# First head pair's queries and keys made by seven block products behind the gates, in a hybrid encoder layer

## The chip, the cores and the metric

The kernel runs on one core of a Trainium2 chip. The metric is the device time of one execution in microseconds. It is the median of three runs for the kernel before: 1119.58 us (1119.29 to 1119.91). A profile is one more execution, with its own time.

## The reference

One layer of a post-norm encoder for 1024 tokens of 1024 channels in float32. It has two sub-layers; the change touches the first, and in it the two branches below.

```python
proj = x @ w_in[l] + b_in[l]
glu_in, q, k, v, gate_logits = jnp.split(proj, splits, axis=-1)
y_conv = conv_branch(glu_in, w_dw[l], b_dw[l], ln_conv_g[l], ln_conv_b[l], w_conv_out[l])
y_attn = chunked_attention(heads(q), heads(k), heads(v), rel_bias[l]) @ w_attn_out[l]
g_conv, g_attn = jnp.split(jax.nn.sigmoid(gate_logits), N_BRANCHES, axis=-1)
mixed = (g_conv * y_conv + g_attn * y_attn) @ w_o[l] + b_o[l]
x = layer_norm(ALPHA * x + mixed, ln1_g[l], ln1_b[l])
x = layer_norm(ALPHA * x + grouped_moe(...), ln2_g[l], ln2_b[l])
```

`conv_branch` is a GLU (512 channels), a causal depthwise convolution of width 31, a LayerNorm over the channels (mean, centring, variance), a swish and a product. `chunked_attention` has 8 heads of 64 channels, a band of 640 key columns for a tile of 128 queries, and a learned bias.

## The kernel before, in words

Every large product is made in three parts, with each operand split in a high and a low half: `mm3` (lines 685 to 687) issues high by high, low by high and high by low. ScalarE makes the high half (`high`, `unit_high`), VectorE or GpSimd subtracts it to get the low half (`low`, `unit_low`, `first_low`, `v_low`, `qk_low`). The order of the work is written out by hand: each engine has its own program, and semaphores tie them.

TensorE's program, in order:

1. Blocks 0 to 7 (128 weight columns each): the GLU halves, `weights_left`. Meanwhile VectorE runs the 31 taps of the convolution, channel block by channel block (`conv_tap`, line 1245), and the last channel block's GLU product is `glu(3)` (line 1229).
2. The gates: 2048 columns as 8 pairs of column blocks. Each pair is made by 7 block products ("units") in place of 8, with sums of weight blocks and of token blocks (Strassen's scheme in Winograd's form). 56 units, `gate_product`, of 12 matmuls each. Each unit needs a weight block of 256 KB in one of 8 slots (`load_unit` on SP's queue), split by ScalarE and by GpSimd (L647). The sums of weight blocks are made by DMAs on GpSimd's queue, from DRAM to DRAM, in rounds: `sums_round(r)` waits until all of round r-1 has landed, and issues the copies (L634) and the accumulating DMAs (L632) of its stages. Rounds 0 to 4 stand before the first `unit_low`; round 5 stands behind that of unit 4, round 6 behind that of unit 9 (`LATE_ROUNDS`). VectorE adds the products up (`gate_sums`, L1289) between taps, ScalarE takes the sigmoid and SP stores the gates.
3. The convolution's mean (`conv_mean`, line 745: two products with ones), then the values of two head pairs in 8 tiles of 24 matmuls (`v_tile`), with the variance (`conv_var`, line 753) ahead of tile 5.
4. Queries and keys of the first head pair, blocks 10 and 11, by 4 `half_sum`s of 24 matmuls of 512 columns.
5. The attention in 32 slots (`scores` L779, `transpose_probs` L793, `weigh_values` L807), with the other pairs' queries and keys, the other values and the convolution's output product between. Then the output products and the mixture of experts.

In stage 3, VectorE centres (line 1367), sums the squares (1259), and makes the low halves of the values (1354). Behind the values come four reciprocals (1376), `normalise` (1349) and the low halves of the first pair (1362). GpSimd makes the low halves of blocks 8 to 11 (L603), scales and masks two bias tiles (`scale_bias`, L609 to L613), then the low halves of blocks 12 and 13. Four PSUM banks serve the value tiles: tile t waits for `v_lo` of tile t-4. Behind the values TensorE waits for the block and for the last tile's low half:

```python
for i in range(2):
    pe.wait_ge(w_lo, B_Q[0] + i + 1)
    pe.wait_ge(v_lo, TT)
```

## Time and profile before

| | |
|---|---|
| median of 3 runs | 1119.58 us (1119.29 to 1119.91) |
| the profiled execution | 1120.55 us, its span 1118.8 us |
| TensorE matmuls | 1081.1 us busy, 97% |
| VectorE, ScalarE, GpSimd | 833.2, 556.9, 365.0 us busy |
| chain that ended last | TensorE 81%, VectorE 6%, DMA 4%, ScalarE 3% |

The span leaves out 1.75 us of the profiled execution. A matmul's duration overlaps with the next one's, so the pace of a series is the distance between starts. A row's time in brackets is the idle time of the engine ahead of it, with what ended it; "issue" stands where nothing in the profile did. In a row with a count, the duration is that of the whole series.

### The profile page before, as it was taken

The page shows a single profiled execution, that of the slowest core. Times are in us where ns is not written, and L with a number is a line of the kernel's source. Part 1 is how long each engine was busy: PE and PEld are TensorE (multiplying, and loading weights), DVE is VectorE, ACT ScalarE, POOL GpSimd, SP SyncE. Part 2 cuts the span into 40 slices and gives each one's busy share as a digit, 9 for nine tenths or more (in the row PEclk, how much of TensorE's full clock was granted, in tenths as well). Part 3 has the DMA queues.
Part 4 walks back from the last instruction along what each step waited for, and adds up shares of the span by engine and source line. Part 5 has one row for each costly group of instructions (what it writes and reads, how often), then busy time and mean ns, then how long its engine had stood idle before and what let it go on. Part 6 is the DMA issues. An engine that isn't in the chain of part 4 may idle for free.

```text
span 1118.8 us, 17230 instructions
## 1 busy us (share of the span) xinstructions
PE 1081.1 (97%) x5487; PEld 897.1 (80%) x5488; DVE 833.2 (74%) x1195; ACT 556.9 (50%) x854; POOL 365.0 (33%) x317
## 2 busy tenths in 40 slices
PE   9999999999999999999999999899999999999984
PEld 7887888888788889788888888788888888888762
DVE  7899999995667766666774688888588646548766
ACT  6412343434476755645330224487487545548764
POOL 2535454444176854667000000024122121112220
PEclk9998999999999999999999999999999999999998
DMA  9898555543201100450750435898999975699966
GB/s 324 252 232 192 162 161 147 159 145 104 75 20 43 31 33 7 183 225 23 269 188 1 157 149 204 304 329 313 377 325 365 317 250 183 205 382 327 348 206 243
DMA packets 60938, 222.68 MB, mean 199 GB/s; under 512 B 9169, under 2 KB 9553, under 8 KB 56770
## 3 DMA queue, kind: packets, MB, share of 16 engines
q1 hardware_dynamic: 51602, 182.49, 44.0%
q0 software_dynamic: 9264, 39.27, 14.5%
q8 instruction: 40, 0.66, 0.2%
q14 instruction: 32, 0.26, 0.1%
HBM read 189.27 MB, written 49.30 MB: 213 GB/s over the span
## 4 chain that ended last, share of the span: by engine, by line
PE 81%; DVE 6%; DMA 4%; ACT 3%; issue 3%; POOL 2%; DVEq 1%; ACTq 0%; SPq 0%; POOLq 0%
PE ps L685 15%; PE ps L687 15%; PE ps L686 15%; PE ps L1823 8%; PE ps L1825 8%; PE ps L1824 8%; PE ps L807 2%; PE ps L793 2%; DMA dn_raw<-in_wexp 2%; DMA gu<-in_wexp 2%; PE ps L779 2%; PE ps L1904 1%; PE ps L1819 1%; POOL pr L597 1%; PE ps L1931 1%
## 5 line engine op out<-in xcount | busy, mean ns | idle before, releaser
L1722 DVE TENSOR_TENSOR gu<-gu (+1 forms) x128 | 148.5, 1219 | 34.7 <-issue 20.8
L1245 DVE SCALAR_TENSOR_TENSOR ps<-u,dw_t,ps 128x1024 f32<-128x1024 f32 x116 | 149.1, 1285 | 2.3
L1823 PE MATMUL ps<-gu,xgh 128*128 x336 | 134.0, 399 | 3.4 <-DVE xgl L2221 2.8
L1716 ACT ACTIVATE gu<-gu (+1 forms) x128 | 124.0, 1047 | 21.7 <-DMA gu<-in_wexp 13.6
L1825 PE MATMUL ps<-gu,xgl 128*128 x336 | 131.7, 392 | 0.0
L1824 PE MATMUL ps<-gu,xgh 128*128 x336 | 131.4, 391 | 0.0
L597 POOL TENSOR_SCALAR pr<-pr,rinv 128x640 f32<-128x640 f32 (+4 forms) x64 | 95.4, 1503 | 77.3 <-DVE rinv L1407 77.1
L685 PE MATMUL ps<-xh,wh 128*128 128x512 f32 x256 | 102.9, 402 | 1.7 <-DVE vhl L1354 1.0
L686 PE MATMUL ps<-xl,wh 128*128 128x512 f32 x256 | 100.0, 390 | 0.0
L687 PE MATMUL ps<-xh,wl 128*128 128x512 f32 x256 | 99.8, 390 | 0.0
L647 POOL TENSOR_TENSOR ul<-uraw,uh 128x512 fp32r<-128x512 f32 x52 | 68.6, 1436 | 71.4 <-ACT uh L1030 71.4
L2316 DVE TENSOR_TENSOR dn_l<-dn_raw,dn_h 128x1024 fp32r<-128x1024 f32 x60 | 69.5, 1219 | 10.9 <-ACT dn_h L2064 10.8
L1823 PEld LDWEIGHTS ps<-gu,xgh 128*128 128x128 f32 x336 | 63.4, 189 | 17.4 <-issue 4.8
L1825 PEld LDWEIGHTS ps<-gu,xgl 128*128 128x128 f32 x336 | 63.4, 189 | 13.5
L1824 PEld LDWEIGHTS ps<-gu,xgh 128*128 128x128 f32 x336 | 63.6, 189 | 12.7
L1823 PE MATMUL ps<-dn_h,hbh 128*128 128x512 f32 x168 | 68.3, 407 | 2.4 <-DVE hbl L2320 2.4
L1760 POOL DMA_INDIRECT acc_rows<-ys,to_now x20 | 37.6, 1880 | 94.0 <-ACT ys L2089 77.6
L1825 PE MATMUL ps<-dn_h,hbl 128*128 128x512 f32 x168 | 66.6, 397 | 0.0
L1824 PE MATMUL ps<-dn_l,hbh 128*128 128x512 f32 x168 | 66.5, 396 | 0.0
L1120 ACT ACTIVATE pr<-pr,nmx 128x640 f32<-128x640 f32 (+4 forms) x64 | 44.1, 690 | 43.8 <-DVE nmx L1398 43.8
L1747 POOL COPY id_now<-ids_i 128x1 int32 (+1 forms) x19 | 11.3, 594 | 164.9 <-PE ps L1904 164.9
L2064 ACT ACTIVATE dn_h<-dn_raw 128x1024 fp32r<-128x1024 f32 x60 | 58.7, 1048 | 8.9 <-DMA dn_raw<-in_wexp 5.2
(308 smaller groups left out, 2662.3 us busy)
## 6 DMA issues: line engine op xcount, KB each, us to landing
gu<-in_wexp SPq DMA_DIRECT2D x64, 1024.0 KB, 8.8
dn_raw<-in_wexp SPq DMA_DIRECT2D x16, 2048.0 KB
raw<-in_wblk SPq DMA_DIRECT2D x36, 512.0 KB, 4.3
gate_weight_sums<-in_wblk POOLq DMA_DIRECT2D x48, 256.0 KB, 6.2
uraw<-gate_weight_sums SPq DMA_DIRECT2D x32, 256.0 KB, 2.9
gate_cols<-gst SPq DMA_DIRECT2D x32, 256.0 KB, 3.3
uraw<-in_wblk SPq DMA_DIRECT2D x24, 256.0 KB, 2.9
xf<-acc_rows SPq DMA_DIRECT2D x8, 512.5 KB, 8.3
```

Source lines behind the costliest of these rows:

```text
L597: pool.tensor_scalar(pr[n % 3][:, h, 0:nt * P], pr[n % 3][:, h, 0:nt * P], rinv[:, n % 3, h:h + 1], None, ALU.mult).then_inc(p_ready, 1)
L647: pool.tensor_tensor(ul[:, s], uraw[:, s], uh[:, s], ALU.subtract).then_inc(u_lo, 1)
L685: pe.matmul(o, a_h, b_h, start=first, stop=False)
L686: pe.matmul(o, a_h, b_l, start=False, stop=False)
L687: return pe.matmul(o, a_l, b_h, start=False, stop=last)
L1245: dve.scalar_tensor_tensor(out=so_far if k < CW - 1 else cv[:, j, :], in0=tap, scalar=w, in1=so_far, op0=ALU.mult, op1=ALU.add).then_inc(c ...
L1716: eng.activation(gu[:, par, k, 0, :], gu[:, par, k, 1, :].bitcast(F32), ACT.Copy).then_inc(gu_hi, 1)
L1722: eng.tensor_tensor(gu[:, par, k, 1, :], gu[:, par, k, 1, :].bitcast(F32), gu[:, par, k, 0, :], ALU.subtract).then_inc(gu_lo, 1)
L1823: pe.matmul(o, a_h, b_h, start=first, stop=False)
L1824: pe.matmul(o, a_h, b_l, start=False, stop=False)
L1825: return pe.matmul(o, a_l, b_h, start=False, stop=last)
L2316: dve.tensor_tensor(dn_l[:, k, :], dn_raw[:, k, :], dn_h[:, k, :], ALU.subtract).then_inc(dn_lo, 1)
```

## The change

The first pair's queries and keys become a ninth pair behind the eight of the gates, so that there are 63 units. Their weight sums are a fifth group of the rounds: round 4 has 4 copies more, round 5 two accumulating DMAs more, round 6 one, and a round 7 with one stands behind unit 14. Their results stand in SBUF (`gst`), not in PSUM; `qk_high` and `qk_low` of the first pair read them there, between the value tiles. The 4 half sums and their two waits go. `conv_mean` stands ahead of unit 59, and `centre`, `square` and `square_sum` between the last units. `conv_var` stands ahead of value tile 2. On VectorE the reciprocals stand behind value tiles 2 and 3, and a `normalise` behind each of tiles 4 to 7. TensorE waits for `v_lo` of all 8 tiles and for the root of the variance ahead of the first scores. `glu(3)` stands ahead of the low halves of units 2 and 3 instead of behind three taps. The slots of the units are turned by one, so that units 1, 3 and 5 wait for one block more. GpSimd splits blocks 8 to 11 and scales both bias tiles; the splits of the second pair's blocks are now those of 10 and 11. The blocks are renumbered, since two are gone.

```diff
-VAR_TILE = 5
+VAR_TILE = 2
 CCE_ROW = 2048
 FIRST_UNITS = 4
-LATE_ROUNDS = {4: 5, 9: 6}
+LATE_ROUNDS = {4: 5, 9: 6, 14: 7}
...
-B_V = (8, 16)
-B_Q = (10, 12, 14, 18)
-B_OC, B_OA, B_WO = 20, 24, 28
-N_BLOCKS = 36
+B_V = (8, 14)
+B_Q = (None, 10, 12, 16)
+B_OC, B_OA, B_WO = 18, 22, 26
+N_BLOCKS = 34
 W_GATE = N_BLOCKS
+GATE_PAIRS = KC
+Q0K0 = KC
+N_PAIRS = KC + 1
...
-UNITS = [(x, q) for q in range(KC) for x in ORDER]
+UNITS = [(x, q) for q in range(N_PAIRS) for x in ORDER]
 N_UNITS = len(UNITS)
+FIRST_SLOT = -N_UNITS % UNIT_SLOTS
...
-    cols += [v, v + 1, q, k, q + 1, k + 1, q + 2, k + 2, v + 2, v + 3, q + 3, k + 3]
-    return cols, [gate + j for j in range(N_GATE)]
+    cols += [v, v + 1, q + 1, k + 1, q + 2, k + 2, v + 2, v + 3, q + 3, k + 3]
+    return cols, [gate + j for j in range(N_GATE)] + [q, k]
...
+        def unit_slot(m):
+
+            return (m + FIRST_SLOT) % UNIT_SLOTS
+
         def sum_round(x, q):
 
             return q // 2 + {5: 1, 7: 1, 6: 2, 3: 3}[x]
 
         def sums_issued(r):
 
-            return sum(2 * many for g in range(KC // 2) for stage, many in enumerate((4, 2, 1, 1)) if g + stage <= r)
+            return sum(pairs_of(g) * many for g in range(SUM_GROUPS) for stage, many in enumerate((4, 2, 1, 1)) if g + stage <= r)
...
-        V_BANKS = (0, 1, 2, 3)
+        FROM_SLOT = (0, 2, 1, 3)
+        V_BANKS = (1, 2, 3, 4)
...
-                        sp.wait_ge(blk_used, B_V[0] - RING + m // 2 + 1)
+                        sp.wait_ge(blk_used, B_V[0] - RING + unit_slot(m) // 2 + 1)
...
-                for n in range(B_V[0], B_Q[0] + 2):
+                for n in range(B_V[0], B_Q[1] + 2):
                     low(n)
                 scale_bias(0)
                 scale_bias(1)
-                for n in range(B_Q[1], B_Q[1] + 2):
-                    low(n)
...
-                    bank_read(N_UNITS - 2)
-                    bank_read(N_UNITS - 1)
                     pe.wait_ge(sum_ok, 2 * (CB - 1))
                     for h in range(2):
-                        last = pe.matmul(ps[:, 4 + h, :], ones[:], sqr[:, 0, HALF * h:HALF * h + HALF], start=True, stop=True)
+                        last = pe.matmul(ps[:, 6 + h, :], ones[:], sqr[:, 0, HALF * h:HALF * h + HALF], start=True, stop=True)
...
+                    if m == N_UNITS - 4:
+                        conv_mean()
                     gate_product(m)
 
-                conv_mean()
...
-                for i in range(2):
-                    pe.wait_ge(w_lo, B_Q[0] + i + 1)
-                    pe.wait_ge(v_lo, TT)
-                    for h in range(2):
-                        half_sum(B_Q[0] + i, h, ps[:, 2 * i + h, :], 0, KC).then_inc(qk_done, 1)
+                pe.wait_ge(v_lo, TT)
+                pe.wait_ge(sq_done, CB + 1)
...
+                def square(j):
+                    act.wait_ge(cent, j + 1)
+                    act.activation(sqr[:, j, :], cv[:, j, :], ACT.Square).then_inc(sq_done, 1)
...
+                    if N_UNITS - 2 <= m < N_UNITS:
+                        square(2 * (m - N_UNITS + 2))
+                        square(2 * (m - N_UNITS + 2) + 1)
...
-                    act.wait_ge(qk_done, i + 1)
-                    act.activation(dst[:, HALF * h:HALF * h + HALF], o, ACT.Identity,
-                                   bias=b_in_t[:, col:col + 1]).then_inc(qk_hi, 1)
-
-                for j in range(CB):
-                    act.wait_ge(cent, j + 1)
-                    act.activation(sqr[:, j, :], cv[:, j, :], ACT.Square).then_inc(sq_done, 1)
+                    if i < 4:
+                        act.wait_ge(blk_used, B_V[0] + N_UNITS)
+                        act.wait_ge(c_sum, sum_no((C11, C12, C21, C22)[i], Q0K0))
+                    else:
+                        act.wait_ge(qk_done, i - 3)
+                    if i in (2, 3):
+                        act.activation(o, o, ACT.Identity, scale=-1.0, bias=b_in_t[:, col:col + 1]).then_inc(sig_ready, 1)
+                        act.wait_ge(sig_ready, CB + len(SIGMOIDS) + i - 1)
+                        act.activation(dst[:, HALF * h:HALF * h + HALF], o, ACT.Copy).then_inc(qk_hi, 1)
+                    else:
+                        act.activation(dst[:, HALF * h:HALF * h + HALF], o, ACT.Identity,
+                                       bias=b_in_t[:, col:col + 1]).then_inc(qk_hi, 1)
+
                 for t in range(TT):
                     v_high(0, t, ps[:, V_BANKS[t % 4], 0:2 * P])
-                    if t == 1:
-                        high(B_Q[0])
+                    if t < 4:
+                        qk_high(t, gst[:, 0, FROM_SLOT[t], :])
                     if t == 3:
-                        high(B_Q[0] + 1)
+                        high(B_Q[1])
+                    if t == 5:
+                        high(B_Q[1] + 1)
                     if t == VAR_TILE:
                         act.wait_ge(stat_done, 2)
-                        act.activation(std[:], psf[:, 4 * HALF:6 * HALF], ACT.Sqrt, scale=1.0 / DC, bias=eps[:]).then_inc(sq_done, 1)
-                high(B_Q[1])
-                high(B_Q[1] + 1)
+                        act.activation(std[:], psf[:, 6 * HALF:8 * HALF], ACT.Sqrt, scale=1.0 / DC, bias=eps[:]).then_inc(sq_done, 1)
                 for j in range(CB):
                     act.wait_ge(nrm, j + 5)
                     act.activation(cv[:, j, :], cv[:, j, :], ACT.Silu, scale=cpar[:, 1, j:j + 1],
                                    bias=cpar[:, 2, j:j + 1]).then_inc(silu_done, 1)
-                for i in range(4):
-                    qk_high(i, ps[:, i, :])
...
+                def centre(j):
+                    dve.wait_ge(stat_done, 1)
+                    dve.scalar_tensor_tensor(out=cv[:, j, :], in0=psf[:, 6 * HALF:8 * HALF], scalar=-1.0 / DC, in1=cv[:, j, :],
+                                             op0=ALU.mult, op1=ALU.add).then_inc(cent, 1)
...
+                    if n == B_V[0] - 1:
+                        glu(CB - 1)
...
-                glu(CB - 1)
                 for m in range(N_UNITS):
                     gate_sums(m)
                     some_taps(1 + (m % 2 or m < 12))
-                assert taps == CB * CW
+                    if N_UNITS - 4 <= m < N_UNITS - 2:
+                        assert taps == CB * CW
+                        centre(2 * (m - N_UNITS + 4))
+                        centre(2 * (m - N_UNITS + 4) + 1)
+                    if m == N_UNITS - 2:
+                        square_sum(1)
+                square_sum(2)
+                square_sum(3)
...
+                    if i in (2, 3):
+                        dve.tensor_tensor(lo[b % 2][:, c], o, hi[b % 2][:, c], ALU.subtract).then_inc(qk_lo, 1)
+                    else:
+                        dve.scalar_tensor_tensor(out=lo[b % 2][:, c], in0=o, scalar=b_in_t[:, col:col + 1],
+                                                 in1=hi[b % 2][:, c], op0=ALU.add, op1=ALU.subtract).then_inc(qk_lo, 1)
+
                 for t in range(TT):
-                    if 1 <= t <= 3:
-                        square_sum(t)
                     v_low(0, t, ps[:, V_BANKS[t % 4], 0:2 * P])
-                dve.wait_ge(sq_done, CB + 1)
-                for i in range(4):
-                    c = slice(2 * P * i, 2 * P * i + 2 * P)
-                    dve.reciprocal(rstdc[:, c], std[:, c]).then_inc(nrm, 1)
-                for j in range(CB):
-                    normalise(j)
-                for i in range(4):
-                    qk_low(i, ps[:, i, :])
+                    if t < 4:
+                        qk_low(t, gst[:, 0, FROM_SLOT[t], :])
+                    if t in (2, 3):
+                        dve.wait_ge(sq_done, CB + 1)
+                        for i in (2 * t - 4, 2 * t - 3):
+                            c = slice(2 * P * i, 2 * P * i + 2 * P)
+                            dve.reciprocal(rstdc[:, c], std[:, c]).then_inc(nrm, 1)
+                    if 4 <= t:
+                        normalise(t - 4)
...
+    def in_ring(i):
+        return i if i < 4 else 4 + (B_WO + i) % RING
```

VectorE's program from the last units' products (L1289, after L1310) to the first scores (ISA). Before:

```order
L1253 TENSOR_TENSOR csum<-csum,cv 128x1024
L1289 TENSOR_TENSOR gst<-ps,gst 128x512
L1367 SCALAR_TENSOR_TENSOR cv<-ps,cv 128x1024 x4
...
L1259 TENSOR_TENSOR sqr<-sqr 128x1024
L1354 TENSOR_TENSOR vhl<-ps,vhl 128x2x128 x5
L1376 RECIPROCAL rstdc<-std 128x256 x4
L1349 TENSOR_TENSOR cv<-cv,rstdc 128x1024 x4
L1362 SCALAR_TENSOR_TENSOR ql_77<-ps,b_in_t,qh_75 128x512 x2
L1362 SCALAR_TENSOR_TENSOR kl_81<-ps,b_in_t,kh_79 128x512 x2
L1398 ISA pr_86,nmx<-ps,bias_84 128x128
```

After the change, from value tile 2 on:

```order
L1388 TENSOR_TENSOR vhl<-ps,vhl 128x2x128
L1397 TENSOR_TENSOR kl_81<-gst,kh_79 128x512
L1410 RECIPROCAL rstdc<-std 128x256 x2
L1388 TENSOR_TENSOR vhl<-ps,vhl 128x2x128
L1397 TENSOR_TENSOR kl_81<-gst,kh_79 128x512
L1410 RECIPROCAL rstdc<-std 128x256 x2
L1388 TENSOR_TENSOR vhl<-ps,vhl 128x2x128
L1383 TENSOR_TENSOR cv<-cv,rstdc 128x1024
...
L1383 TENSOR_TENSOR cv<-cv,rstdc 128x1024
L1388 TENSOR_TENSOR vhl<-ps,vhl 128x2x128
L1383 TENSOR_TENSOR cv<-cv,rstdc 128x1024
L1430 ISA pr_86,nmx<-ps,bias_84 128x128
```

Where the 8 value tiles' subtractions stood ahead of the reciprocals and of `normalise`, four reciprocals and three `normalise` (L1383) now stand ahead of the last of them.

GpSimd's program from the first low half of a unit (L664) to the first probabilities (L614), after the change:

```order
L664 TENSOR_TENSOR ul<-uraw,uh 128x512
L649 DMA gate_weight_sums<-in_wblk 32x2048 x2
L649 DMA gate_weight_sums<-gate_weight_sums 32x2048 x4
L664 TENSOR_TENSOR ul<-uraw,uh 128x512 x5
L649 DMA gate_weight_sums<-gate_weight_sums 32x2048 x3
...
L620 TENSOR_TENSOR wl<-raw,wh 128x1024 x4
L626 TENSOR_SCALAR bias_84<-bias_84 128x1280
...
L626 TENSOR_SCALAR bias_85<-bias_85 128x1280
...
L614 TENSOR_SCALAR pr_86<-pr_86,rinv 128x128 x2
```

Between the low halves of units 4 and 5 there were four DMAs, and are now six. The two block splits that stood behind the bias tiles are now the last two of the four ahead of them.

## Rows read from the trace of the kernel before

**Rows 1.** The page: the chain that ended last, shares of the span by engine.

```profile
PE 81%; DVE 6%; DMA 4%; ACT 3%; issue 3%; POOL 2%; DVEq 1%; ACTq 0%; SPq 0%; POOLq 0%
```

**Rows 2.** Timeline of PE: from unit 53 to the first value tile.

```profile
245.42 0.39 PE L685 MATMUL ps<-xh,uh 128*128 128x512 f32 x1
...
253.35 0.39 PE L687 MATMUL ps<-xraw_r,ul 128*128 128x512 f32 x1
254.93 1.96 PE L745 MATMUL ps<-csum,ones 128*128 128x512 f32 x4 [1.18 <-DVE csum L1253]
256.32 0.69 PE L685 MATMUL ps<-wh,xh 128*128 128x256 f32 x1
256.84 0.28 PE L686 MATMUL ps<-wl,xh 128*128 128x256 f32 x1
```

**Rows 3.** Timeline of PE: first half sum of the first pair, and first scores.

```profile
282.64 0.47 PE L685 MATMUL ps<-xh,wh 128*128 128x512 f32 x1 [1.03 <-DVE vhl L1354]
...
304.58 0.33 PE L779 MATMUL ps<-kh,qh 64*128 64x128 f32 x2
```

**Rows 4.** Timeline of PE, then stretches of 5 us with the granted clock (PEclk), at units 1 and 2.

```profile
103.68 0.77 PE L685 MATMUL ps<-t_h,uh 128*128 128x512 f32 x1 [2.70 <-issue]
...
100.00:105.00 5.00, 2.30 (x8) 1.65 (x7) 4.93 (x5) 0.88 (x2) 1.62 (x3) 0.80 0.97 283
105.00:110.00 5.00, 5.00 (x13) 3.89 (x13) 4.96 (x6) 1.51 (x3) 5.00 (x7) 0.52 0.88 143
```

**Rows 5.** Timeline of DVE at the same place.

```profile
97.26 1.28 DVE L1263 TENSOR_TENSOR ul<-uraw,uh 128x512 fp32r<-128x512 f32 x2
...
102.30 1.28 DVE L1229 SCALAR_TENSOR_TENSOR u<-ps,b_in_t,sig 128x1024 f32<-128x1024 f32 x1
```

**Rows 6.** Timeline of POOL: rounds 3 to 5 of the weight sums.

```profile
66.44 3.92 POOL L634 DMA_DIRECT2D gate_weight_sums<-in_wblk  x8 [10.45 <-DMA gate_weight_sums<-gate_weight_sums]
...
89.34 3.16 POOL L632 DMA_DIRECT2D gate_weight_sums<-in_wblk  x4 [12.57 <-DMA gate_weight_sums<-gate_weight_sums]
...
99.57 1.29 POOL L647 TENSOR_TENSOR ul<-uraw,uh 128x512 fp32r<-128x512 f32 x1 [3.89 <-ACT uh L1030]
104.24 3.21 POOL L632 DMA_DIRECT2D gate_weight_sums<-gate_weight_sums  x4 [3.38 <-DMA gate_weight_sums<-gate_weight_sums]
106.33 3.67 POOL L647 TENSOR_TENSOR ul<-uraw,uh 128x512 fp32r<-128x512 f32 x2
```

**Rows 7.** Timeline of ACT in the value tiles: one tile, the root, a block's high half.

```profile
268.43 0.39 ACT L1084 ACTIVATE vhl<-ps 128x256 fp32r<-128x256 f32 x1 [2.50 <-PE ps L687]
...
276.30 1.28 ACT L1106 ACT_TABLE_LOAD   x1
277.59 1.11 ACT L1106 ACTIVATE std<-ps,eps 128x1024 f32<-128x1024 f32 x1
...
286.62 1.06 ACT L1020 ACTIVATE wh<-raw 128x1024 fp32r<-128x1024 f32 x1 [0.20 <-DMA raw<-in_wblk]
```

**Rows 8.** Timeline of DVE, reciprocals and `normalise`; then the latter's own durations (min/median/max).

```profile
282.41 6.58 DVE L1376 RECIPROCAL rstdc<-std 128x256 f32<-128x256 f32 x4
289.02 6.80 DVE L1349 TENSOR_TENSOR cv<-cv,rstdc 128x1024 f32<-128x1024 f32 x4
...
L1349 DVE TENSOR_TENSOR cv<-cv,rstdc x4: 1210/1211/3398, 289.0 to 294.6; 128x1024 f32<-128x1024 f32 x4
```

**Rows 9.** Timeline of POOL: a bias tile and two block splits.

```profile
272.31 3.47 POOL L609 TENSOR_SCALAR bias<-bias 128x1280 f32<-128x1280 f32 x1
...
286.57 4.76 POOL L603 TENSOR_TENSOR wl<-raw,wh 128x1024 fp32r<-128x1024 f32 x2 [6.17 <-ACT wh L1020]
```

**Rows 10.** DVE and POOL at a late split, and POOL's pair of the same size earlier.

```profile
460.67 2.67 DVE L1215 TENSOR_TENSOR wl<-raw,wh 128x1024 fp32r<-128x1024 f32 x1
...
462.24 2.80 POOL L597 TENSOR_SCALAR pr<-pr,rinv 128x256 f32<-128x256 f32 x2
...
310.09 1.83 POOL L597 TENSOR_SCALAR pr<-pr,rinv 128x256 f32<-128x256 f32 x2 [0.27 <-DVE rinv L1407]
```

More of the change, by code:

```diff
@@ L312, in wait_used @@
             elif n < B_OC:
-                b, i = [(b, n - B_Q[b]) for b in range(PAIRS) if 0 <= n - B_Q[b] < 2][0]
-                eng.wait_ge(qk_done, 1 + max(p for p in range(4 * PAIRS) if qk_of(p)[:2] == (b, i)))
+                b, i = [(b, n - B_Q[b]) for b in range(1, PAIRS) if 0 <= n - B_Q[b] < 2][0]
+                eng.wait_ge(qk_done, -3 + max(p for p in range(4 * PAIRS) if qk_of(p)[:2] == (b, i)))
             elif n < B_OA:
@@ L331, in gate_weights, with pairs_of @@
             return whole[P * DC * k:P * DC * k + P * DC]
+        SUM_GROUPS = (N_PAIRS + 1) // 2
+        def pairs_of(g):
+            return min(2, N_PAIRS - 2 * g)
+        def unit_slot(m):
+            return (m + FIRST_SLOT) % UNIT_SLOTS
         def sum_round(x, q):
@@ L359, in sigmoids_at @@
             x, q = UNITS[m - 2]
+            if q == Q0K0:
+                return []
             return [(q, slot) for after, slot in ((7, 3), (2, 0), (3, 2), (4, 1)) if after == x]
@@ L421, in oc_pieces @@
             return of
-        SPLITS = {1: (14,), 2: (15,), 5: (16,), 9: (17,), 13: (18,), 17: (19,), 25: (20,), 27: (21,), 29: (22,), 30: (23,),
-                  31: (24,), 32: (25,), 33: (26,)}
+        SPLITS = {1: (12,), 2: (13,), 5: (14,), 9: (15,), 13: (16,), 17: (17,), 25: (18,), 27: (19,), 29: (20,), 30: (21,),
+                  31: (22,), 32: (23,), 33: (24,)}
         UO_SLOTS = {23: (0,), 24: (1, 2), 25: (3,)}
@@ L543, in _ @@
                     if n == B_OA - 2:
-                        sp.wait_ge(qk_done, 4 * PAIRS)
+                        sp.wait_ge(qk_done, 4 * (PAIRS - 1))
                         sp.wait_ge(v_done, 2 * TT)
@@ L621, in weight_sums @@
                 def weight_sums(g, stage):
-                    if not 0 <= g < KC // 2:
+                    if not 0 <= g < SUM_GROUPS:
                         return
-                    for q in (2 * g, 2 * g + 1):
+                    for q in range(2 * g, 2 * g + pairs_of(g)):
                         s1, s2, s3, s4 = (wsum_dram[i, q] for i in range(4))
@@ L643, in unit_low @@
                 def unit_low(m):
-                    s = m % UNIT_SLOTS
+                    s = unit_slot(m)
                     pool.wait_ge(u_hi, m + 1)
@@ L720, in gate_product @@
                     x, q = UNITS[m]
-                    s, bank = m % UNIT_SLOTS, unit_bank(m)
+                    s, bank = unit_slot(m), unit_bank(m)
                     pe.wait_ge(u_lo, m + 1)
@@ L898, in qk_sum @@
                         pe.wait_ge(w_lo, B_Q[b] + i + 1)
-                        if p == 5:
-                            pe.wait_ge(cent, CB)
-                        elif p not in (4, 15):
+                        if p not in (4, 5, 15):
                             pe.wait_ge(qk_lo, p)
@@ L1261, in first_low @@
                 def first_low(m):
+                    s = unit_slot(m)
                     dve.wait_ge(u_hi, m + 1)
-                    dve.tensor_tensor(ul[:, m], uraw[:, m], uh[:, m], ALU.subtract).then_inc(u_lo, 1)
+                    dve.tensor_tensor(ul[:, s], uraw[:, s], uh[:, s], ALU.subtract).then_inc(u_lo, 1)
                 def input_sums():
@@ L1361, in qk_low @@
                     dve.wait_ge(qk_hi, i + 1)
-                    dve.scalar_tensor_tensor(out=lo[b % 2][:, c], in0=o, scalar=b_in_t[:, col:col + 1],
-                                             in1=hi[b % 2][:, c], op0=ALU.add, op1=ALU.subtract).then_inc(qk_lo, 1)
-                dve.wait_ge(stat_done, 1)
-                for j in range(CB):
-                    dve.scalar_tensor_tensor(out=cv[:, j, :], in0=psf[:, 6 * HALF:8 * HALF], scalar=-1.0 / DC, in1=cv[:, j, :],
-                                             op0=ALU.mult, op1=ALU.add).then_inc(cent, 1)
+                    if i in (2, 3):
[3 more added lines that the diff above has]
+                                                 in1=hi[b % 2][:, c], op0=ALU.add, op1=ALU.subtract).then_inc(qk_lo, 1)
                 for t in range(TT):
-                    if 1 <= t <= 3:
-                        square_sum(t)
                     v_low(0, t, ps[:, V_BANKS[t % 4], 0:2 * P])
-                dve.wait_ge(sq_done, CB + 1)
-                for i in range(4):
-                    c = slice(2 * P * i, 2 * P * i + 2 * P)
-                    dve.reciprocal(rstdc[:, c], std[:, c]).then_inc(nrm, 1)
-                for j in range(CB):
-                    normalise(j)
-                for i in range(4):
-                    qk_low(i, ps[:, i, :])
+                    if t < 4:
[7 more added lines that the diff above has]
+                        normalise(t - 4)
                 for i in range(2):
@@ L2431, in halves_apart @@
         return b.reshape(-1, P, 2, CB * P).transpose(0, 2, 1, 3).reshape(-1, P, KC, P)
+    def in_ring(i):
+        return i if i < 4 else 4 + (B_WO + i) % RING
     first, gates = block_columns()
     w_in = columns(w_in)
-    blocks = np.concatenate([w_in[first], two_a_block(w_conv_out), two_a_block(w_attn_out), columns(w_o), halves_apart(w_in[gates])])
+    blocks = np.concatenate([w_in[first], two_a_block(w_conv_out), two_a_block(w_attn_out), columns(w_o)[[in_ring(i) for i in range(KC)]], halves_apart(w_in[gates])])
     rel = np.clip(np.arange(P)[:, None] - np.arange(BANDW)[None, :] + 512, -256, 256) + 256
```

10 lines of the change are left out of this document (5 added, 5 removed).

## The prediction, made before the result was known

> **What bounds the kernel now.** The page first: the chain that ended last runs through TensorE for 81% of the span and through VectorE for 6% [rows 1]. So every matmul removed is time won, and every idle stretch of TensorE is time lost, as long as nothing takes its place. Next TensorE's timeline around the change. The units run without a gap: from 245.42 to 253.35 there are 35 steps, 0.2266 us each [rows 2], so a unit of 12 matmuls is 2.72 us. Before the mean TensorE waits from 253.58 to 254.93, 1.35 us; the mean's products hold the next matmul off for 1.39 us and leave it 0.4 us longer (0.69 against 0.28) [rows 2]: 1.8 us. Behind the values there is a wait of 1.03 us, and the 96 matmuls of the first pair run from 282.64 to 304.58, 21.94 us [rows 3]. One more wait lies near the beginning, ahead of unit 2: 2.70 us [rows 4], for glu(3), which starts at 102.30 [rows 5]. There the granted clock then falls to 0.52 for 105 to 110 us [rows 4], the 1.2 GHz level: 13 matmuls start where 22 (5 / 0.2266) would. TensorE had been idle for 2.70 us before. By the starts, the 1.2 GHz level lasts from 103.68 to about 109.9: 6.2 us, of which half, 3.1 us, is lost.
>
> **The change, part by part.** Times in the values are counted from the start of the first value tile.
>
> 1. Products. Seven units more: 84 x 0.2266 = +19.0 us. Four half sums less: -21.9 us.
>
> 2. The mean stands ahead of unit 59, seven units behind the last tap, so its wait of 1.35 us goes; its 1.8 us stay. The centring, the squares and their sums then lie beside four units (10.9 us), and in the first 3 us of the values. VectorE's taps end at unit 54 as before, so this is covered. -1.35 us.
>
> 3. The beginning. glu(3) would start at 97.26, where the low halves of units 2 and 3 start now [rows 5], and these follow by 99.8; unit 2 is due at 100.8. The wait of 2.70 goes. What is late next is unit 5. GpSimd makes the low half of unit 4 at 99.57, then waits for round 4 until 104.24, issues four DMAs in 2.1 us, and makes unit 5's [rows 6]. Today that is hidden, since TensorE is late itself. Without that lateness, unit 5 is due at 100.8 + 3 x 2.72 = 109.0. Round 4 gets four copies more. Their price: at least the 2.0 us that issuing takes (3.92 for eight); at most 4.0, half of what separates round 3 (eight copies and eight accumulations, 66.44 to 89.34, 22.9 us) from round 4 (eight accumulations, 89.34 to 104.24, 14.9 us) [rows 6]. I take the middle, 3.0: landed at 107.2. Then six DMAs instead of four, 3.15 us, and 1.3 us for the low half: unit 5 starts at 111.8, an idle time of 2.8 us (1.8 to 3.8). It is as long as the one removed, so I let the clock fall as today: +0.1 us in sum (-4 to +1).
>
> 4. Turned slots: the loads of units 1, 3 and 5 start one block (10.9 us) later. Unit 5's is issued at 95.6 and shares the queues with round 4; it is covered by the wait for that round. Nothing, as long as part 3 holds. The blocks of the second pair are needed only in the first slots of the attention, and are split by then.
>
> 5. The end of the values, the large term. Tiles follow one another by 2.88 us (ScalarE's 0.39 and the 2.50 it waits [rows 7]); eight, with the variance's 1.8 us ahead of the third, end at 24.9. Tile 2 ends at 10.4. ScalarE takes its high half (0.4), then two passes over 512 columns of the keys (about 1.3, from 1.06 for 1024 columns [rows 7], twice), and loads a table and takes the root (1.28 and 1.11 [rows 7]): done at 14.6. From there VectorE has, ahead of tile 7's low half, four reciprocals (6.58 us), three passes of normalise (1.21 each, 1.13 start to start) [rows 8], and six small subtractions (2.3 us): 14.6 + 6.6 + 3.4 + 2.3 = 26.9. That alone makes TensorE wait 2.1 us behind tile 7.
>
> But GpSimd works at the same time. Today one normalise takes 3.40 us instead of 1.21: it starts at 289.02 and ends when GpSimd's second split (286.57 + 4.76 = 291.33 [rows 9]) plus 1.1 us is over [rows 8]. The two engines take turns by whole instructions where VectorE reads both inputs from SBUF. It works the other way too: a VectorE split held at 460.67 until 462.26 runs to 463.3, and GpSimd's pair of tensor_scalar at 462.24 takes 2.80 us instead of 1.83 [rows 10]. So I expect GpSimd's bias tiles, tensor_scalar of 3.47 us [rows 9], to hold normalise likewise.
> The order then is: block 10's split, 17.1 to 19.5, holds the keys' low half from 18.2 (ends 20.2); two reciprocals and tile 4's low half, to 23.8; block 11's split, 20.6 to 23.0; bias tile 0, 23.0 to 26.5. The first normalise waits for it and ends at 27.6; bias tile 1 has the turn until 31.1; the second normalise ends at 32.2, the third at 33.7, tile 7's low half at 34.1. TensorE starts at 34.2 and has been idle for 9.3 us, where it was 1.03: +8.3 us. Bounds: 2.1 us of idle time with no holding, 11 if a normalise more is held.
>
> The Trainium skill (SBUF — State Buffer, on the shared port pair) states this as a rule: the pair is an exclusive lock, kept for the whole instruction, between any GpSimd operation that reads SBUF and a VectorE operation with two SBUF inputs. This case's trace agrees for GpSimd's tensor_tensor (3.40 us against 1.21); for a VectorE operation behind tensor_scalar no row here shows it.
>
> 6. The clock. An idle stretch of 2.70 us was followed by 6.2 us at 1.2 GHz [rows 4]; those of 1.03 and 1.18 us [rows 2, 3] were not. Behind 9.3 us it will fall. Cost: at most the 3.1 us of that row; nothing if it stays. I take 2.6. The attention's first slots have little slack to hide it, so it counts in full.
>
> Sum: 19.0 - 21.9 - 1.35 + 0.1 + 8.3 + 2.6 = **+6.8 us**. The profiled execution is 1120.55 us (span 1118.8), 0.97 above the median of the runs; the forecast for the median is 1119.58 + 6.8 = 1126.4 us.
>
> **Rivals.**
> - *tensor_scalar does not hold VectorE.* Then only the two splits do: tile 7's low half is done at about 28.4, and TensorE waits 3.5 us. 19.0 - 21.9 - 1.35 + 0.1 + 2.5 = -1.7; the clock gives 0 to +3.1. About 1119.3 (1117.5 to 1121). For it: no row has this pair in this direction. Against: rows 10 in the other.
> - *The beginning comes free.* Round 4's copies fill gaps of the DMA queues and land by 104.5, or the idle time ahead of unit 5 does not lower the clock: 3.0 to 5.8 us less, with the rest as forecast: 1120.6 to 1123.4. Against: round 3 shows no free room behind its copies.
> - *Faster: VectorE is held by nobody in the values.* Place: tile 7's low half. If the splits and bias tiles fall between its two-input operations, the wait behind the values is 2.1 us, only 1.1 more than today, and the clock stays: 19.0 - 21.9 - 1.35 + 0.1 + 1.1 = -3.0, 1116.6 us. It decides at an idle time of about 4 us, from which the saved 4.2 us (parts 1 and 2) are used up. Against: the bias tiles and the last three normalise are due in the same 8 us.
> - *It does not do what it says:* the waits of the attention's first slots only move and take the saving back. TensorE has no slack there to give, so I fold this into the range.
>
> **Numbers.** Forecast 0.56, own range 1123.5 to 1129.5. Unheld by tensor_scalar 0.20, of it 0.14 within the bound, 0.04 faster, 0.02 slower. Beginning free 0.12, of it 0.08 slower, 0.04 same. Unheld at all 0.12, faster. A measurement of this kernel tells 0.2% (2.2 us) from no change. Slower 0.66, same 0.18, faster 0.16. The range of 1117.5 to 1129.5 leaves out most of the last rival and what lies above: some 0.18.
>
> **What would show it.** In the new profile: an idle time of TensorE ahead of unit 5 instead of unit 2, near 109 us, ended by GpSimd; none ahead of the mean; behind the values an idle time near 9 us ended by VectorE's low half (L1388), with two passes of L1383 of 4 us or more that end 1.1 us behind a bias tile; a clock below 0.8 in the 5 us behind it. Wrong: passes of L1383 all near 1.2 us, a wait of 2 to 4 us, or first scores less than 30 us behind the first value tile.

## The result and the profile after

The changed kernel takes 1131.22 us (median of 5 runs, 1130.67 to 1133.95), the kernel before on the same chip 1119.91: a ratio of 1.01, 95% interval 1.0081 to 1.0119. Slower, as forecast, but by 11.3 us instead of 6.8, and outside the range, which ended at 1129.5. The profiled execution took 1131.88 us, 11.33 above that of before.

The page of the changed kernel, chain that ended last; its shares now make 73% in all, so they can't be set against [rows 1]. Then its list of TensorE's longest waits (total, times, longest). The second was in no term of the sum; 2.0 of its 6.7 us are in the kernel before too.

```profile
PE 58%; DVE 5%; DMA 4%; ACT 2%; issue 2%; POOL 2%; ACTq 0%; DVEq 0%; SPq 0%; POOLq 0%
```

```profile
PE ps L792 <- DVE vhl L1388: 8.2, 1, 8.2
PE ps L1936 <- issue: 6.7, 2, 4.7
PE ps L700 <- POOL ul L664: 6.1, 1, 6.1
```

**The beginning** (against [rows 4] and [rows 6]). Timeline of PE, then of POOL, then PE's stretches of 5 us with the granted clock (the 0.79 and 0.53 behind the busy times):

```profile
115.31 0.79 PE L700 MATMUL ps<-xh,uh 128*128 128x512 f32 x1 [6.13 <-POOL ul L664]
```

```profile
90.70 1.50 POOL L651 DMA_DIRECT2D gate_weight_sums<-in_wblk  x3 [12.13 <-DMA gate_weight_sums<-gate_weight_sums]
...
101.13 1.29 POOL L664 TENSOR_TENSOR ul<-uraw,uh 128x512 fp32r<-128x512 f32 x1 [1.92 <-DVE ul L1284]
109.16 1.61 POOL L649 DMA_DIRECT2D gate_weight_sums<-in_wblk  x2 [6.74 <-DMA gate_weight_sums<-gate_weight_sums]
110.21 3.75 POOL L649 DMA_DIRECT2D gate_weight_sums<-gate_weight_sums  x4
112.24 7.94 POOL L664 TENSOR_TENSOR ul<-uraw,uh 128x512 fp32r<-128x512 f32 x5
```

```profile
110.00:115.00 5.00, 0.00 (x0) 0.00 (x0) 4.93 (x6) 1.50 (x3) 5.00 (x8) 0.79 1.07 256
115.00:120.00 5.00, 4.69 (x12) 3.69 (x13) 4.93 (x6) 1.97 (x3) 5.00 (x5) 0.53 0.89 180
```

The wait ahead of unit 2 is gone, and one of 6.13 us stands ahead of unit 5, ended by GpSimd. GpSimd got round 4's data at 109.16, issued six DMAs until 113.96 (110.21 + 3.75), and only then made the low half that unit 5 needs: its record starts at 112.24, but it ends at 115.25, 1.3 us behind the last issue. Behind the wait the clock is 0.53, the 1.2 GHz level, as it was behind the 2.70 us of before.

**The mean** (against [rows 2]). Timeline of PE: no wait stands ahead of it any more; the products hold the next matmul off for 1.32 us.

```profile
264.14 0.39 PE L702 MATMUL ps<-t_h,ul 128*128 128x512 f32 x1
264.37 1.88 PE L760 MATMUL ps<-csum,ones 128*128 128x512 f32 x4
265.69 0.80 PE L700 MATMUL ps<-t_h,uh 128*128 128x512 f32 x1
...
277.02 0.28 PE L700 MATMUL ps<-wh,xh 128*128 128x256 f32 x1
```

**The end of the values** (against [rows 3], [rows 8] and [rows 9]). Timelines of PE, DVE and POOL, and the granted clock around it:

```profile
310.16 0.47 PE L792 MATMUL ps<-kh,qh 64*128 64x128 f32 x2 [8.24 <-DVE vhl L1388]
```

```profile
300.63 3.57 DVE L1383 TENSOR_TENSOR cv<-cv,rstdc 128x1024 f32<-128x1024 f32 x1
304.12 0.41 DVE L1388 TENSOR_TENSOR vhl<-ps,vhl 128x256 fp32r<-128x256 f32 x1
304.46 3.84 DVE L1383 TENSOR_TENSOR cv<-cv,rstdc 128x1024 f32<-128x1024 f32 x1
308.22 0.41 DVE L1388 TENSOR_TENSOR vhl<-ps,vhl 128x256 fp32r<-128x256 f32 x1
308.56 1.21 DVE L1383 TENSOR_TENSOR cv<-cv,rstdc 128x1024 f32<-128x1024 f32 x1
309.69 0.41 DVE L1388 TENSOR_TENSOR vhl<-ps,vhl 128x256 fp32r<-128x256 f32 x1
```

```profile
300.10 3.46 POOL L626 TENSOR_SCALAR bias<-bias 128x1280 f32<-128x1280 f32 x1
...
304.23 3.45 POOL L626 TENSOR_SCALAR bias<-bias 128x1280 f32<-128x1280 f32 x1
```

```profile
305.00:310.00 5.00, 0.00 (x0) 0.00 (x0) 5.00 (x4) 1.91 (x3) 3.07 (x3) 0.50 0.25 102
310.00:315.00 5.00, 4.84 (x17) 3.95 (x18) 2.07 (x8) 4.45 (x7) 0.28 (x1) 0.57 0.01 3
```

Two passes of `normalise` take 3.57 and 3.84 us instead of 1.21. Each ends some 0.6 us behind a bias tile (303.56 and 307.68), so most of its time passed beside GpSimd's `tensor_scalar`. Tile 7's low half, behind the third pass, is what TensorE waits for, 8.24 us.

**The tail**, which the prediction did not speak of. Timeline of PE at the first transposes behind the expert loop, of the changed kernel, then of the kernel before:

```profile
1062.56 0.87 PE L1936 MATMUL ps<-ident_t,xg 128*128 128x128 f32 x6 [2.05 <-issue]
1068.08 0.59 PE L1936 MATMUL ps<-ident_t,xg 128*128 128x128 f32 x2 [4.65 <-issue]
```

```profile
1056.33 1.09 PE L1904 MATMUL ps<-ident_t,xg 128*128 128x128 f32 x8 [2.01 <-issue]
```

The eight transposes, one group in the kernel before, are cut by 4.65 us in which TensorE waits for nothing that the profile shows ("issue"). The clock falls behind it:

```profile
1065.00:1070.00 5.00, 1.44 (x4) 0.96 (x4) 1.27 (x2) 1.75 (x4) 0.00 (x0) 0.52 0.20 79
```

The lateness against before grows from 6.2 us at the first transpose (1062.56 and 1056.33) to 11.3 at the end (spans of 1130.1 and 1118.8). The list of DMA queues suggests a cause. In the stretch from 1063 to 1068.1 of the changed kernel, and in that from 1056 to 1062 of the kernel before, one block moves on a queue of instructions (packets, MB, share):

```profile
q8 instruction: 1, 0.02, 1.3%
```

```profile
q8 instruction: 1, 0.02, 1.1%
```

So the transfer alone is no sign: it is there in both kernels, and only one is cut. What can differ is how soon TensorE needs the block. The queue moved 41 blocks, 0.67 MB, so 16 KB each, and in straight stretches of the program one comes about every 250 to 270 of the matmuls and weight loads recorded; that it is TensorE's code is inferred from this. The change took 24 such instructions out of TensorE's program and added 4 that only wait. So the ends of the blocks lie 20 instructions later in the code of the tail.

### The profile page after: what moved, and what is told of

It reads as the page before. It is cut to its first block, busy times and chain, and to the rows that moved or that the text cites. A ratio compares the mean times of both kernels' runs of the same rounds, so it can differ in the third digit from the quotient of the medians.

```text
span 1130.1 us, 17255 instructions
## 1 busy us (share of the span) xinstructions
PE 1079.2 (95%) x5475; PEld 895.8 (79%) x5476; DVE 840.0 (74%) x1202; ACT 560.8 (50%) x862; POOL 367.9 (33%) x330
## 4 chain that ended last, share of the span: by engine, by line
PE 58%; DVE 5%; DMA 4%; ACT 2%; issue 2%; POOL 2%; ACTq 0%; DVEq 0%; SPq 0%; POOLq 0%
PE ps L1855 9%; PE ps L1857 9%; PE ps L1856 9%; PE ps L700 7%; PE ps L702 7%; PE ps L701 7%; PE ps L820 2%; PE ps L806 2%; DMA dn_raw<-in_wexp 2%; PE ps L792 2%; DMA gu<-in_wexp 2%; PE ps L1936 1%; PE ps L1851 1%; POOL pr L614 1%; PE ps L1963 1%
## 5 line engine op out<-in xcount | busy, mean ns | idle before, releaser
L614 POOL TENSOR_SCALAR pr<-pr,rinv 128x640 f32<-128x640 f32 (+4 forms) x64 | 95.2, 1500 | 67.9 <-DVE rinv L1439 67.7
L664 POOL TENSOR_TENSOR ul<-uraw,uh 128x512 fp32r<-128x512 f32 x59 | 78.5, 1489 | 73.3 <-ACT uh L1039 71.4
L700 PE MATMUL ps<-xh,wh 128*128 128x512 f32 x224 | 91.1, 407 | 1.0 <-DVE xl L1240 0.6
L701 PE MATMUL ps<-xl,wh 128*128 128x512 f32 x224 | 88.0, 393 | 0.0
L702 PE MATMUL ps<-xh,wl 128*128 128x512 f32 x224 | 87.9, 392 | 0.0
```

Of the source, the lines that this page charges most:

```text
L614: pool.tensor_scalar(pr[n % 3][:, h, 0:nt * P], pr[n % 3][:, h, 0:nt * P], rinv[:, n % 3, h:h + 1], None, ALU.mult).then_inc(p_ready, 1)
L664: pool.tensor_tensor(ul[:, s], uraw[:, s], uh[:, s], ALU.subtract).then_inc(u_lo, 1)
L700: pe.matmul(o, a_h, b_h, start=first, stop=False)
L701: pe.matmul(o, a_h, b_l, start=False, stop=False)
L702: return pe.matmul(o, a_l, b_h, start=False, stop=last)
```

## The experiments

Ten kernels; each was timed beside the kernel before on its own chip, whose median was 1119.7 to 1120.4 us. The ratio need not be that of the two medians.

| kernel | median, us | range | ratio to before (95%) |
|---|---|---|---|
| a_pad2 | 1125.14 | 1124.31 to 1129.83 | 1.0062 (1.0034 to 1.0090) |
| b_short2 | 1125.48 | 1122.26 to 1128.81 | 1.0046 (1.0028 to 1.0065) |
| d_short | 1129.87 | 1127.60 to 1133.87 | 1.0089 (1.0074 to 1.0105) |
| a_bias2 | 1127.51 | 1121.87 to 1132.26 | 1.0068 (1.0049 to 1.0088) |
| a_late2 | 1125.18 | 1123.93 to 1127.17 | 1.0047 (1.0030 to 1.0064) |
| a_nocopy2 | 1124.21 | 1123.46 to 1131.07 | 1.0044 (1.0025 to 1.0064) |
| b_best2 | 1120.45 | 1115.12 to 1124.11 | 1.0000 (0.9984 to 1.0015) |
| c_three2 | 1113.52 | 1111.20 to 1120.16 | 0.9938 (0.9919 to 0.9957) |
| c_four2 | 1113.89 | 1112.38 to 1115.63 | 0.9943 (0.9928 to 0.9959) |
| d_glu | 1118.74 | 1115.94 to 1125.10 | 1.0000 (0.9984 to 1.0016) |

### Where the blocks of TensorE's code end: a_pad2, b_short2, d_short

```diff
 # a_pad2, the changed kernel
-                pe.wait_ge(zero_ok, 1)
+                for _ in range(41):
+                    pe.wait_ge(zero_ok, 1)
 # b_short2, the kernel before, and d_short, the changed one
-                for _ in range(7):
-                    pe.matmul(ps[:, 7, 0:2 * P], zeros[:, 0:P], zeros[:, 0:2 * P], start=True, stop=True)
+                for _ in range(3):
+                    pe.matmul(ps[:, 7, :], zeros[:, 0:P], zeros[:, 0:HALF], start=True, stop=True)
```

Expected of a_pad2: 

> The changed kernel with 40 further waits on an already raised semaphore ahead of TensorE's warm-up, which make 20 instructions: as many as the change took out of TensorE's program (24 matmul and weight-load instructions fewer, 4 waits more). Nothing else differs. Theory A (code position): the 4.65 us idle time inside the 8 transposes behind the expert loop (L1936) comes from a 16 KB block of TensorE's own program being fetched there; with the old block boundaries it is gone, the transposes run as 8 in one piece, and the run takes 4 to 7 us less than the changed kernel (1131.2), about 1125.5. Theory B (it belongs to the data or to transfers at that time): the idle time stays, 1131 us.

Expected of b_short2: 

> The kernel before, with three warm-up products of 512 columns instead of seven of 256: 16 instructions of TensorE fewer, nearly as short as the changed kernel (20 fewer). Theory A (code position): the transposes behind the expert loop (L1904) are now split by an idle time of 3 to 6 us, and the kernel before becomes 4 to 7 us slower, about 1125, though nothing it computes has changed. Theory B: no idle time there, 1119.6 us within 1 us.

Expected of d_short: 

> The changed kernel with three warm-up products of 512 columns instead of seven of 256: 16 instructions of TensorE fewer again, so 36 fewer than before. By the two splits seen (16 fewer: behind 4 of the 8 transposes; 20 fewer: behind 6) the block's end now lies 6 products behind the transposes. Theory A (the next block is fetched only when TensorE has come near it, so a short stretch behind the loop's exit does not hide it): the transposes run in one piece, and an idle time of 3 to 4.6 us stands inside the products at L1855 to L1857 behind them; total as the changed kernel, 1129 to 1131. Theory B (only the jump itself and what lies right behind it is hurt): no idle time, about 1125.

Timeline of PE at the same transposes, of a_pad2, of b_short2 (the kernel before, 16 instructions shorter) and of d_short (the changed one, 16 shorter again):

```profile
1060.91 1.09 PE L1937 MATMUL ps<-ident_t,xg 128*128 128x128 f32 x8 [2.21 <-issue]
```

```profile
1057.34 0.65 PE L1904 MATMUL ps<-ident_t,xg 128*128 128x128 f32 x4 [2.27 <-issue]
1062.59 1.01 PE L1904 MATMUL ps<-ident_t,xg 128*128 128x128 f32 x4 [4.60 <-issue]
```

```profile
1065.28 1.09 PE L1936 MATMUL ps<-ident_t,xg 128*128 128x128 f32 x8 [2.19 <-issue]
1066.34 0.47 PE L1855 MATMUL ps<-dn_h,hbh 128*128 128x512 f32 x1
1066.65 0.40 PE L1856 MATMUL ps<-dn_l,hbh 128*128 128x512 f32 x1
1066.88 0.40 PE L1857 MATMUL ps<-dn_h,hbl 128*128 128x512 f32 x1
1071.14 0.80 PE L1855 MATMUL ps<-dn_h,hbh 128*128 128x512 f32 x1 [3.86 <-issue]
```

The cut moves with the length of the code ahead of it: none at the old length, behind 4 transposes at 16 instructions fewer, behind 6 at 20, and behind all 8 and 3 recorded products at 36 (I expected 6; I take it that instructions which are no matmul stand between). It doesn't move with the time: in a_bias2, a_late2 and a_nocopy2 below, whose TensorE program is as long as the changed kernel's, it stands behind 6 transposes too, though these come 5 to 8 us earlier. In all the kernels of this document the instruction queue moved 41 blocks where there is a cut, and 40 where there is none.

Where the block moves, found with windows of 0.1 us of the DMA list (times in us):

| kernel | block at the loop's exit | first transpose | next block | TensorE goes on behind the cut |
|---|---|---|---|---|
| before | 1053.7 | 1056.33 | 1059.5 | no cut |
| a_pad2 | 1058.3 | 1060.91 | 1064.2 | no cut |
| changed | 1059.9 | 1062.56 | 1065.8 | 1068.08 |
| b_short2 | 1054.7 | 1057.34 | 1060.3 | 1062.59 |
| d_short | 1062.7 | 1065.28 | 1068.6 | 1071.14 |

The next block moves 2.9 to 3.3 us behind the first transpose in all five, whether TensorE needs it or not. Where there is a cut, TensorE goes on 2.3 to 2.6 us behind that, so 5.3 to 5.9 us behind the first transpose. A block that ends within so short a stretch behind the loop's exit leaves TensorE idle for the rest of it; one that ends later costs nothing here.

The kernel before, shorter by four warm-up products and otherwise the same, becomes 5.1 us slower, and its profiled execution loses 7.4 us between two steps on either side of this place (0.8 us late at 1037.20, 8.1 at 1092.31). Theory A stands. The median of a_pad2 is 6.1 us below the changed kernel's, but not all of that belongs to the tail. In the profiled executions, 7.1 us apart, 1.65 are there at the first transpose already: round 4 was over at 107.12 instead of 109.16, unit 5 was due 1.0 us later for TensorE's late start, and so the wait ahead of unit 5 was 3.1 us instead of 6.13. The other 5.4 lie in the tail. The 2.0 to 2.5 us ahead of the transposes, at the exit of the loop, are there in every kernel, and a block moves 2.6 to 2.7 us ahead of the first transpose.

### What holds `normalise`: a_bias2

```diff
-                for n in range(B_V[0], B_Q[1] + 2):
+                for n in range(B_V[0], B_Q[1]):
                     low(n)
                 scale_bias(0)
                 scale_bias(1)
+                for n in range(B_Q[1], B_Q[1] + 2):
+                    low(n)
```

Expected: 

> The changed kernel with GpSimd's two bias tiles ahead of the splits of blocks 10 and 11 instead of behind them. Theory A (tensor_scalar on GpSimd holds VectorE's normalise): all passes of normalise take 1.2 us or wait for a split alone, the idle time behind the values falls from 8.24 us to 3 to 5 us, with it perhaps the fall of the clock (2 us): 1124 to 1128 us. Rival (VectorE is merely late, or held by something else): idle time and time stay, 1131 us.

All four passes of `normalise` (min/median/max in ns), TensorE's wait, and what VectorE does beside the first bias tile: a low half of the values, with an operand in PSUM, and the new victim, the low half of the queries, with two operands in SBUF (it took 0.75 us in the changed kernel):

```profile
L1385 DVE TENSOR_TENSOR cv<-cv,rstdc x4: 1204/1207/1207, 299.4 to 303.8; 128x1024 f32<-128x1024 f32 x4
```

```profile
PE ps L794 <- DVE vhl L1390: 3.3, 1, 3.3
```

```profile
282.04 0.42 DVE L1390 TENSOR_TENSOR vhl<-ps,vhl 128x256 fp32r<-128x256 f32 x1 [1.52 <-ACT vhl L1102]
282.65 2.02 DVE L1401 SCALAR_TENSOR_TENSOR ql<-gst,b_in_t,qh 128x512 fp32r<-128x512 f32 x1 [0.19 <-ACT qh L1119]
```

```profile
281.10 3.47 POOL L626 TENSOR_SCALAR bias<-bias 128x1280 f32<-128x1280 f32 x1 [10.28 <-DMA bias<-in_relb]
```

The wait falls by 4.9 us, and the held operation is another one, which nobody waits for. The median falls by 3.7 us; the runs of a_bias2 scatter over 10 us, so the size rests on the wait, and the direction on both. That `tensor_scalar` holds VectorE is shown: by the two long passes of the changed kernel, by their going with the order, and by the new victim, which ends at 284.67, just behind the bias tile's 284.57. The low half with an operand in PSUM, at 282.04 inside the same bias tile, takes 0.42 us as it does elsewhere and is not held. The Trainium skill (SBUF — State Buffer, on the shared port pair) has this as an exclusive lock for the whole instruction. That VectorE is held, the rows here agree with. How long, they leave open by half a microsecond: the passes end 0.6 us behind the bias tile where 1.21 are needed, the low half 0.10 behind where 0.75 are, as if the lock ended 0.6 us ahead of the tile's recorded end; recorded spans of GpSimd are rough.

### What unit 5 waits for: a_late2, a_nocopy2

```diff
 # a_late2
-LATE_ROUNDS = {4: 5, 9: 6, 14: 7}
+LATE_ROUNDS = {9: 5, 14: 6, 19: 7}
 # a_nocopy2
-            return min(2, N_PAIRS - 2 * g)
+            return 2 if g < KC // 2 else 0
...
-                    of = wsum_dram[SUMS[x], q] if x in SUMS else gate_weights(q, *PARTS[x])
+                    of = wsum_dram[SUMS[x], q % KC] if x in SUMS else gate_weights(q, *PARTS[x])
```

Expected of a_late2: 

> The changed kernel with rounds 5, 6 and 7 of the weight sums behind the low halves of units 9, 14 and 19 instead of 4, 9 and 14. Theory A (round 5's wait and its six DMA issues hold the low half of unit 5): the idle time of 6.1 us ahead of unit 5 goes, with the clock's fall behind it: 6 to 8 us less, 1123 to 1125 us, unless a later load finds its sum not ready. Rival 1 (unit 5 is late for its own load, shared with round 4): the idle time stays in part. Rival 2 (the time is given back at units 6 and 7, which are late too): 2 to 4 us less.

Expected of a_nocopy2: 

> The changed kernel without the weight sums of the ninth pair (its units load the first pair's sums instead, so queries and keys of the first head pair are other numbers): round 4 has no copies and round 5 four DMAs instead of six. Theory (copies 3.6 us, two DMA issues 1.6 us of the 6.1 us ahead of unit 5): the idle time falls to about 1 us (up to 2), the clock stays, 1124 to 1126. Rival (what holds round 4 is the loads of the units, turned by one slot): it stays above 4 us.

In a_late2 TensorE has no wait at all between 95 and 262 us, and the first scores start at 302.00 instead of 310.16, behind the same wait of 8.24 us: 8.2 us won, 6.1 of wait and the rest clock. The median is 6.0 us lower. Timeline of POOL of a_nocopy2:

```profile
87.87 3.16 POOL L649 DMA_DIRECT2D gate_weight_sums<-in_wblk  x4 [10.73 <-DMA gate_weight_sums<-gate_weight_sums]
...
102.16 3.21 POOL L649 DMA_DIRECT2D gate_weight_sums<-gate_weight_sums  x4 [0.94 <-DMA gate_weight_sums<-gate_weight_sums]
104.24 7.43 POOL L664 TENSOR_TENSOR ul<-uraw,uh 128x512 fp32r<-128x512 f32 x5
```

a_nocopy2 leaves out the ninth pair's weight sums. Without their copies round 4 lasts 14.3 us (87.87 to 102.16) instead of 18.5 (90.70 to 109.16), and the wait is gone. In the kernels with round 5 behind unit 4, round 4 takes 17.9 to 18.5 us with the copies (changed, a_pad2, a_bias2, d_short), and 14.3 to 14.9 without (before, b_short2, a_nocopy2), so the copies cost 3.0 to 4.2 us. Of the 7.0 us by which round 4 is over earlier here, 2.8 are chance: round 3, the same in both, ended that much earlier. The loads of the units, turned by one slot here too, are not what holds it.

### Whether the beginning counts: b_best2, d_glu

b_best2 is the kernel before with glu(3) ahead of the low halves and the rounds later; c_three2 is the changed kernel with the edits of a_late2 and a_bias2 and 20 TensorE instructions more; d_glu is c_three2 with glu(3) back in its old place.

```diff
 # b_best2
-LATE_ROUNDS = {4: 5, 9: 6}
+LATE_ROUNDS = {9: 5, 14: 6}
...
+                    if n == B_V[0] - 1:
+                        glu(CB - 1)
...
-                glu(CB - 1)
 # c_three2, in place of 7 x 256 columns; and the edits of a_late2 and a_bias2
+                for _ in range(12):
+                    pe.matmul(ps[:, 7, 0:150], zeros[:, 0:P], zeros[:, 0:150], start=True, stop=True)
 # d_glu: c_three2 with
-                    if n == B_V[0] - 1:
-                        glu(CB - 1)
...
+                glu(CB - 1)
```

Expected of b_best2: 

> The kernel before, without the ninth pair, with glu(3) ahead of the low halves of units 2 and 3 and rounds 5 and 6 of the weight sums behind units 9 and 14. The wait of 2.70 us ahead of unit 2 and the clock's fall behind it go, and none comes ahead of unit 5: 3 to 6 us below before, 1114 to 1117. If c_three is then at 1112, the ninth pair with its mean inside the units is worth 2 to 4 us of its own (4.2 us less its longer wait behind the values); if b_best is at c_three's time or below, it is worth nothing.

Expected of c_three2: 

> The changed kernel with three edits together: rounds 5 to 7 of the weight sums behind units 9, 14 and 19; the bias tiles ahead of the splits of blocks 10 and 11; and 12 warm-up products of 150 columns instead of 7 of 256, which are 20 instructions more at the same time in columns. If the three losses are separate (start 7.9 us, end of values 4.9 us, code position 6 us, by the profiles of the three single runs), they add up: 1131.2 - 18.8 = 1112.4 us, 7 to 9 us below the kernel before. If two of them are one loss (the clock's fall behind a wait counted twice), 1116 to 1119.

Expected of d_glu: 

> c_three with glu(3) back behind the low halves of units 2 and 3, where the kernel before has it. Theory (the start counts in full, because the mean no longer stands right behind VectorE's last tap): TensorE waits 2.7 us ahead of unit 2 and the clock falls behind it, and nothing takes it back: 3 to 6 us above c_three (1113.5), 1116.5 to 1119.5. Rival (VectorE paces the units up to their end here too, as it did when the start of the kernel before was mended and the time came back ahead of the mean): c_three's time within 1 us.

b_best2 gained nothing, against my expectation of 3 to 6 us. Its only wait of TensorE between 95 and 262 us, and the two stretches of before around the units in which VectorE (third busy time) can be read:

```profile
PE ps L745 <- DVE csum L1253: 3.7, 1, 3.7
```

```profile
140.00:160.00 20.00, 20.00 (x90) 16.55 (x89) 19.79 (x20) 7.03 (x12) 9.87 (x7) 1.00 0.50 147
...
200.00:220.00 20.00, 20.00 (x90) 16.57 (x89) 19.75 (x21) 7.99 (x14) 9.26 (x8) 1.00 0.50 147
```

VectorE is busy for 19.8 of 20 us through the units. What TensorE gains at the beginning it mostly loses at the mean, right behind the last tap: it waits 3.7 us instead of 1.18, and the clock, 1.00 there in the kernel before, falls to 0.59 and 0.72 in the 10 us around it. The mean still starts 2.97 us earlier (251.96 beside 254.93), the first scores only 0.2 (304.38 beside 304.58). So in the kernel before the 2.70 us were free. With the mean seven units behind the last tap they are not: c_three2 is at 1113.52, and giving glu(3) back its old place costs 5.2 us by the medians, 0.6% by the ratios to before (d_glu, a wait of 3.0 us ahead of unit 2), and 4.1 us at the first scores of the profiled executions. The three losses add up: 1131.22 - 1113.52 = 17.7 us, expected 18.8 (six runs of c_three2, over 9 us).

### The rest of the wait: c_four2

```diff
-                    if 4 <= t:
-                        normalise(t - 4)
+                for j in range(CB):
+                    normalise(j)
```

Expected: 

> As c_three, and the four passes of normalise behind the low halves of all value tiles instead of between those of tiles 4 to 7. Theory: what is left of the wait behind the values (3.3 us) is three passes of normalise of 1.21 us ahead of tile 7's low half; it falls to about 1 us or less: 2 to 3 us below c_three, about 1110. Rival: normalise comes later, so the activations, splits and output products of the convolution are late in the attention and take it back: c_three's time.

TensorE's waits in c_four2 between 290 and 320 us:

```profile
PE ps L794 <- DVE nmx L1432: 1.5, 1, 1.5
PE ps L794 <- DVE vhl L1390: 0.9, 1, 0.9
PE ps L808 <- POOL pr L614: 0.7, 1, 0.7
```

The wait for the values falls from 3.3 to 0.9 us as expected, but the first maxima now stand behind four passes of `normalise` on VectorE, and TensorE waits for them (1.5 us) and for the probabilities (0.7). The rival was right that it is taken back and wrong about where. The medians do not differ (1113.52 and 1113.89); in one profiled execution of each c_four2 was 2.2 us ahead through the attention, so a small gain stays possible.

## Why the prediction was wrong

By the profiled executions of the kernel before and the changed one:

- **Parts 1 and 2 (products, mean): right.** The wait ahead of the mean is gone and the 96 half-sum matmuls too. From the first value tile to the first scores it was 48.26 us, now 33.14: -21.9 for the half sums, +7.2 of wait, and 0.4 less in the tiles.
- **Part 3 (beginning): right mechanism, too small.** The first value tile came 20.70 us later; 19.0 are the units, -1.35 the mean's wait, so the beginning cost 3.05 us instead of 0.1. Unit 5 was due at 109.18 (forecast 109.0) and started at 115.31 (forecast 111.8). Of the 3.5 us, 1.4 are that round 3 itself ended at 90.70 instead of 89.34, 0.6 that the copies took 3.6 and not 3.0, and some 1.6 the six DMAs: from 109.16 to 115.31 are 6.15 us, less 1.3 for the low half 4.8, so 0.8 a DMA. I took 0.52, the distance between their starts. This was a misreading: the durations in [rows 6] give 0.8 (3.21 us for four), and two low halves behind them took 3.67 us, not 2 x 1.29. The idle time of 6.13 us lies outside my 1.8 to 3.8. The 1.4 us are chance: in a_bias2, d_short and a_pad2, with the same rounds, round 3 ended at 90.02, 89.03 and 88.95, and the wait ahead of unit 5 was 5.6, 4.0 and 3.1 us.
- **Part 4 (turned slots): right** (a_nocopy2 has them, and no wait).
- **Part 5 (end of values): right.** 8.24 us idle, forecast 9.3, +7.2 instead of +8.3; two passes held by the two bias tiles, by 2.4 and 2.6 us, and over 0.6 us behind them, not 1.1. The rival "does not hold" falls with a_bias2.
- **Part 6 (clock): right.** It fell behind the wait, and lateness grew by 1.8 us from the first scores (+5.6) to the first transposes of the attention (+7.4, 318.87 beside 311.44); I took 2.6.
- **What failed: the sum had no term for the length of TensorE's program.** After the attention the changed kernel was 7.4 us late, at the first transpose of the tail 6.2, beside a forecast of 6.8. That these lie so close is in part luck: the beginning was 3.0 us too cheap, the end of the values 1.1, the clock 0.8 and the tiles 0.4 too dear, and 1.2 us came back in the mixture of experts, for which there was no term. Then came 5.1 us in the tail, from the cut inside the transposes and the clock behind it. The step "seven units more, four half sums less" counted 12 matmuls less as time alone. They also moved the rest of the code against its 16 KB blocks, and I looked neither at the idle times called "issue" (2.01 us at the loop's exit of the kernel before) nor at where instruction blocks move. Moving the code costs the kernel before 5.1 us (b_short2). With the old positions restored the changed kernel takes 1125.14 us (a_pad2), inside the range.

The rival "the beginning comes free" was the wrong way round: it cost more. "Nobody held" is excluded by the 3.57 and 3.84 us.

## What to carry to other kernels

Before a change is judged by a few microseconds, look for idle times of the busiest engine called "issue" behind a loop's exit. Here such a loss depended on how many instructions stood ahead, came and went with edits elsewhere, and could be tried with a few idle instructions at the start. Put GpSimd's long operations where VectorE has an operand in PSUM (0.42 us, not held) or works on something that nobody waits for. And ask of every wait that you remove which engine paces the stretch behind it: the same 2.70 us were worth nothing while the mean stood behind VectorE's last tap, and 5.2 once it stood elsewhere; with its three losses mended the changed kernel is 6.9 us faster than before (1113.52 beside 1120.44).
